# Retention values as a fifth seven-product unit, gate tiles ahead of the stage, and the retention's square sums taken off GpSimd

## What is computed

```python
for l in range(DEPTH):                                   # DEPTH = 2
    x = x + 0.5 * swiglu(rmsnorm(x, norm_ffn1[l]), ...)  # D_FF = 2816
    h = rmsnorm(x, norm_mix[l])
    z = h @ w_in[l]                                      # 1024 x 9728
    rq, rk, rv, rg, dq, dk, dv, g_ret, g_dil = jnp.split(z, IN_SPLITS, axis=-1)
    y_ret = retention(rq, rk, rv, rg, ...) @ w_ret_o[l]  # 4 heads, keys of 128, values of 256
    y_dil = dilated_attention(dq, dk, dv, ...) @ w_dil_o[l]   # 3 groups of 4 heads of 128
    gates = sigmoid(concatenate([g_ret, g_dil], axis=-1) + b_gate[l])
    x = x + (gates[..., :1024] * y_ret + gates[..., 1024:] * y_dil) @ w_out[l]
    x = x + 0.5 * swiglu(rmsnorm(x, norm_ffn2[l]), ...)
# at the end of retention(), for each head:
o = o * lax.rsqrt(jnp.mean(o * o, axis=-1, keepdims=True) + EPS)
return silu(g) * (o * norm_g)
```

## Time and profile before

| what | us |
|---|---|
| median of 3 runs | 2577.52 |
| the profiled execution | 2577.28 |
| its span, first to last instruction | 2575.5 |
| TensorE matmul busy | 2567.7 (100%) |
| VectorE busy | 1936.4 (75%) |
| ScalarE busy | 1121.0 (44%) |
| GpSimd busy | 128.5 (5%) |

### The profile page before, as it was taken

The page is one execution under the profiler, slowest core; times in us unless marked ns, Lnnn a source line. Parts: engine busy times, 40 slices in busy tenths (PEclk is TensorE's granted clock), DMA queues, the critical chain, the costliest instruction groups (busy, mean ns, idle before and its releaser), DMA issues.

```text
span 2575.5 us, 36835 instructions
## 1 busy us (share of the span) xinstructions
PE 2567.7 (100%) x14577; PEld 2255.3 (88%) x14577; DVE 1936.4 (75%) x2430; ACT 1121.0 (44%) x1369; POOL 128.5 (5%) x199
## 2 busy tenths in 40 slices
PE   9999999999999999999999999999999999999999
PEld 7999988888888888999989999888888888889998
DVE  8877866886776679777788777777867766797776
ACT  5433444445655234333443334454466642343332
POOL 1111000110001000000000000011100000000000
PEclk9999999999999999999999999999999999999999
DMA  5433245545443433333223332454554434333331
GB/s 183 150 124 119 66 141 191 175 161 175 138 139 115 164 103 119 103 102 98 99 83 123 98 98 74 173 178 147 172 155 139 138 128 151 115 115 98 103 107 52
DMA packets 201202, 328.98 MB, mean 128 GB/s; under 512 B 15572, under 2 KB 122497, under 8 KB 200525
## 3 DMA queue, kind: packets, MB, share of 16 engines
q1 hardware_dynamic: 186312, 286.35, 34.9%
q0 software_dynamic: 14112, 36.50, 3.9%
q10 hardware_dynamic: 646, 4.31, 0.4%
HBM read 289.11 MB, written 42.64 MB: 129 GB/s over the span
## 4 chain that ended last, share of the span: by engine, by line
PE 99%; DVE 0%; DMA 0%; issue 0%; ACT 0%; ACTq 0%
PE proj L692 23%; PE proj L694 23%; PE proj L693 23%; PE acc L693 9%; PE acc L692 9%; PE acc L694 9%; PE acc L1062 1%; PE acc L988 1%; PE acc L1011 0%; PE acc L970 0%; PE acc L971 0%; PE acc L972 0%; PE acc L1001 0%; PE acc L1000 0%; PE acc L765 0%; PE acc L759 0%
## 5 line engine op out<-in xcount | busy, mean ns | idle before, releaser
L692 PE MATMUL proj<-h_hi,ring_hi 128*128 128x256 f32 (+1 forms) x1632 | 553.4, 339 | 1.8 <-DVE h_lo L1791 1.8
L694 PE MATMUL proj<-h_hi,ring_lo 128*128 128x256 f32 (+1 forms) x1632 | 544.6, 334 | 0.0
L693 PE MATMUL proj<-h_lo,ring_hi 128*128 128x256 f32 (+1 forms) x1632 | 543.7, 333 | 0.0
L692 PE MATMUL proj<-y_hi,ring_hi 128*128 128x256 f32 (+1 forms) x1472 | 450.5, 306 | 0.0
L694 PE MATMUL proj<-y_hi,ring_lo 128*128 128x256 f32 (+1 forms) x1472 | 450.5, 306 | 0.0
L693 PE MATMUL proj<-y_lo,ring_hi 128*128 128x256 f32 (+1 forms) x1472 | 450.5, 306 | 0.0
L1262 ACT ACTIVATE ring_hi<-raw 128x1024 fp32r<-128x1024 f32 (+1 forms) x175 | 209.9, 1203 | 360.3 <-PE acc L694 194.6
L692 PEld LDWEIGHTS proj<-h_hi,ring_hi 128*128 128x128 f32 x1632 | 310.3, 190 | 31.4 <-DVE ring_lo L2572 2.2
L694 PEld LDWEIGHTS proj<-h_hi,ring_lo 128*128 128x128 f32 x1632 | 309.9, 190 | 31.2
L693 PEld LDWEIGHTS proj<-h_lo,ring_hi 128*128 128x128 f32 x1632 | 310.4, 190 | 27.5
L692 PEld LDWEIGHTS proj<-y_hi,ring_hi 128*128 128x128 f32 x1472 | 281.3, 191 | 12.5
(11 more groups left out here) (335 smaller groups left out, 4309.6 us busy)
## 6 DMA issues: line engine op xcount, KB each, us to landing
raw<-in_w_in SPq DMA_DIRECT2D x120, 512.0 KB, 4.7
raw<-in_ffn_gate SPq DMA_DIRECT2D x88, 512.0 KB, 3.7
raw<-in_ffn_up SPq DMA_DIRECT2D x88, 512.0 KB, 4.3
raw<-in_ffn_down SPq DMA_DIRECT2D x56, 512.0 KB, 4.4
qkv_d<-work POOLq DMA_DIRECT2D x72, 256.0 KB, 2.6
work<-in_ffn_down SPq DMA_DIRECT2D x32, 512.0 KB, 5.9
xs<-qkv_d SPq DMA_DIRECT2D x24, 512.0 KB, 6.3
xs<-in_w_in SPq DMA_DIRECT2D x16, 512.0 KB, 5.2
```

The lines of the kernel that those rows point to most:

```text
L692: pe.matmul(o, s_hi, m_hi, start=start, stop=False, skip_group_check=onto)
L693: pe.matmul(o, s_hi, m_lo, start=False, stop=False, skip_group_check=onto)
L694: return pe.matmul(o, s_lo, m_hi, start=False, stop=stop, skip_group_check=onto)
```

## The change

Four things are changed.

- The two blocks of retention values leave the cover and become a fifth unit of seven products, the first of the stage. The cover has one plain block left, and behind it three single tiles of the dilated gates (blocks 2, 4 and 6), which the heads 1 to 3 no longer make: those heads have seven tiles. `norm_sums` stands after 24 matmuls of the cover, `norm_spread` after 48. The results and sums of the cover live in `xs`.
- The small products of heads 1 to 3 are put at other k steps, and the heads' PSUM banks go round.
- `ret_normed`, `ret_gated`, `ret_low` and `ret_out` of the previous head stand at the end of a head, not in its middle; so does the split of the next head's first weights on VectorE.
- The sum of the squares is made by VectorE (`ret_sq_add`), its high part by ScalarE (`ret_sq_high`), its low part by VectorE in the next head (`ret_sq_low`).

```diff
-COVER_BLOCKS, ST_UNITS = 3, 4
-ST_BASE = 2 * COVER_BLOCKS
+ST_BASE, ST_UNITS = 5, 5
+COVER_TILES = (NB, NB, 1, 1, 1)
+COVER_GATES = (2, 4, 6)
+HEAD_TILES = ((2, 2, 2, 2), (2, 2, 1, 2), (2, 2, 1, 2), (2, 2, 1, 2))
...
 SyncE, cover
+                sp.wait_ge(ssq_added, 3 * (N + 1))
+                st_block(l, st_b22[0], 4, ST_COLS[1], b22_landed[0])
+                sp.wait_ge(norm_sum, N + 1)
+                st_block(l, st_b12[0], 0, ST_COLS[1], b12_landed)
...
                 split_of(item + ST_BASE - 2)
                 st_block(l, st_b11, 0, ST_COLS[0], b11_landed)
...
 GpSimd, head
-                pool.wait_ge(ret_o_read, 4 * H + 2)
-                pool.tensor_tensor(ret_sq[0], ret_sq[0], ret_sq[1], ALU.add).then_inc(ret_sq_added, 1)
...
-                pool.tensor_copy(hi, ret_sq[0]).then_inc(ret_sq_hi, 1)
-                pool.wait_ge(ret_sq_hi, H + 1)
-                pool.tensor_tensor(lo, ret_sq[0], hi.bitcast(fp32), ALU.subtract).then_inc(ret_sq_lo, 1)
...
 TensorE, cover
+                        if part == 0 and b == 1:
+                            norm_sums(N)
+                    if part == 0:
+                        norm_spread(N)
+                for b, bank in enumerate((AB[2], AB[3], PB[0])):
+                    u = unit(l, 2 + b)
+                    begin(u)
...
+                    tile_cols(u, bank, 0, width=P)
...
 TensorE, heads 1 to 3
-                    between = ({2: [scores(0), scores(1)]}, {0: [scores(2), scores(3)], 1: [total]}, {2: [move]}, {},
-                               {0: [turn(0), turn(1)], 5: [turn(2), turn(3), values(0), values(1)]},
-                               {1: [values(2), values(3), near_values], 5: [rs(0)]})
+                    between = ({2: [scores(0), scores(1)]}, {0: [scores(2), scores(3)], 1: [total]}, {2: [move]},
+                               {2: [turn(0), turn(1)], 7: [turn(2), turn(3), values(0), values(1)]},
+                               {3: [values(2), values(3), near_values], 7: [rs(0)]})
...
+                    between += ({2: [rs(1)], 3: [kq(0)], 5: [rv(0), rs(2)], 6: [kq(1)]},
+                                {0: [rv(1), rs(3)], 2: [rv(2)], 3: [kq(2)], 4: [kq(3)], 5: [rv(3)], 6: [kq(4)], 7: [kq(5)]})
...
 ScalarE, new
+            def ret_sq_high(H, n):
+                act.wait_ge(ret_sq_added, H + 1)
+                act.wait_ge(ret_pv, 4 * H + 4)
+                act.activation(pt_split(y_hi_flat, n, 0), ret_sq[0], ACT.Copy).then_inc(ret_sq_hi, 1)
...
+            def cover_sigmoid(l, b):
+                act.wait_ge(sxn_ready, SXN * l + KT + b + 1)
...
 ScalarE, end of a head
+                turned(4)
                 ret_squares(H, 0)
                 ret_squares(H, 1)
+                turned(5)
+                gate_silu(H, 0, at(3).tile)
+                if n:
+                    ret_out(H - 1, n - 1, 0)
+                    ret_out(H - 1, n - 1, 1)
                 ret_copy(H, n, 0)
                 ret_copy(H, n, 1)
                 gate_silu(H, 1, at(3).tile + 1)
+                ret_sq_high(H, n)
...
 VectorE, new
+            def ret_sq_add(H):
+                dve.wait_ge(ret_o_read, 4 * H + 2)
+                dve.tensor_tensor(ret_sq[0], ret_sq[0], ret_sq[1], ALU.add).then_inc(ret_sq_added, 1)
...
+            def ret_sq_low(H, n):
+                dve.wait_ge(ret_sq_hi, H + 1)
+                dve.tensor_tensor(pt_split(y_lo_flat, n, 0), ret_sq[0], pt_split(y_hi_flat, n, 0).bitcast(fp32),
+                                  ALU.subtract).then_inc(ret_sq_lo, 1)
...
+            def cover_scale(l, b):
+                done(unit(l, 2 + b).tile)
+                dve.wait_ge(cover_stored[b], 16 * (2 * l + 1))
+                dve.tensor_tensor(cover_gate[b], (AB[2], AB[3], PB[0])[b][:, :], r_b[:, :], ALU.mult).then_inc(sxn_ready, 1)
...
 VectorE, end of a head
                 if more:
                     qk_scale(H + 1)
+                split(at(4))
+                if n:
+                    ret_normed(H - 1)
+                    ret_gated(H - 1)
+                    ret_low(H - 1, n - 1)
+                ret_sq_add(H)
...
 VectorE, merge
                 split(at(M_R0))
+                ret_sq_low(H, RET_HEADS - 1)
                 gated_d(0)
                 gated_d(1)
                 ret_mean(H)
```

More of the change, by code:

```diff
@@ L109, in piece_tile @@
 def piece_tile(layer, u, j):
[L110 removed]
+    return layer * TILES_LAYER + FFN_TILES + sum(COVER_TILES) + 2 * (PROD * u + j)
 def ffn_item(layer, f):
@@ L278, in build, with last_use, head_gates, sg_before @@
         ret_sq = [work[:, 12, :], work[:, 13, :]]
-        t_r, t_seed, t_var, t_b = work[:, 12, :], work[:, 13, :], work[:, 15, :], xs[:, 6, :]
+        t_a, t_seed, t_var, t_b = work[:, 12, :], work[:, 13, :], work[:, 15, :], xs[:, 6, :]
+        t_r = t_var
+        HEAD_BANKS = ((0, 1, 2, 3, 1, 2, 3, 0), (1, 2, 3, 0, 1, 2, 3), (0, 1, 2, 3, 0, 1, 2), (3, 0, 1, 2, 3, 0, 1))
+        def last_use(n, tile):
+            before = [(n - 1, t) for t in range(len(HEAD_BANKS[n - 1]))] if n else []
+            before += [(n, t) for t in range(tile)]
+            return next((h, t) for h, t in reversed(before) if HEAD_BANKS[h][t] == HEAD_BANKS[n][tile])
+        def head_gates(n):
+            return ((0, 0), (1, 0), (0, 1), (1, 1)) if n == 0 else ((0, 2 * n), (0, 2 * n + 1), (1, 2 * n + 1))
+        def sg_before(H):
+            return GATES_OF[RET_HEADS] * (H // RET_HEADS) + GATES_OF[H % RET_HEADS]
+        def sg_uses(H, buffer):
+            n = H % RET_HEADS
+            return (2 * H if buffer == 0 else (RET_HEADS + 1) * (H // RET_HEADS) + n + (n > 0))
+        def head_bank(n, tile):
+            return PB[HEAD_BANKS[n][tile]]
         GD, GR = ([work[:, k, :] for k in of] for of in ((4, 5, 6, 7, 1, 1, 13, 15), (8, 9, 14, 0, 12, 2, 3, 10)))
@@ L376, in two_cols128, with col128 @@
                          (v[:, :, :, P:2 * P], w[:, ds(layer, 1), :, ds(col1, P)])])
+            def col128(u, w, layer, col):
+                v = slot(u, KT * P).rearrange("p o (k c) -> p o k c", c=P)
+                load(u, [(v[:, :, k:k + 4, :], w[:, ds(layer, 1), k:k + 4, ds(col, P)]) for k in (0, 4)])
             def cols512(u, w, layer, col, k0=0):
@@ L1647, in heads @@
                     split(at(2))
+                    dil_exps(H, 2)
+                    dil_exps(H, 3)
+                    swap_halves(H, 1, at(0).tile + 1)
+                    rope_hi(H, 0)
+                    dil_factors(H)
+                    gate_sigmoid(l, n, 0)
+                    gate_sigmoid(l, n, 1)
+                    dil_copy(H, 0)
+                    dil_copy(H, 1)
+                    rope_hi(H, 1)
+                    split(at(3))
+                    dil_copy(H, 2)
+                    dil_copy(H, 3)
+                    dil_out(H, n)
+                    squares(0, 2)
+                    gate_sigmoid(l, n, 2)
+                    scores_hi(H, n, 0)
+                    gate_sigmoid(l, n, 3)
                 else:
```

315 lines of the change are left out of this document (159 added, 156 removed).

## The result

The changed kernel takes **2613.20 us** (median of 4 runs, 2610.39 to 2617.14) against 2577.47 for the kernel before: 1.0140 of its time, 95% interval 1.0122 to 1.0157. It is slower, as forecast, by 35.7 us instead of 22.7, and the time lies 1.2 us above the end of the stated range. The profiled execution took 2610.39 us, 33.1 more than that of before.

The account below looks back on a forecast made before the run. TensorE, 99% of the chain, was taken to bound the kernel: waits of 16.8 us a layer, 33.6 in two, against 10.9 saved gave +22.7, so 2600 us against the median; range 2576 to 2612.

Parts of the forecast that it names:

- what goes: TensorE, both layers: 24 fewer matmuls a layer, 48 in all at 0.2267 us each, saving 10.9 us.
- The sign that went with it: TensorE's matmul busy time should be about 11 us lower in the changed kernel.
- norm sums: Cover: sums now stand after 24 matmuls, so TensorE waits 1.2 us for VectorE's last addition of squares.
- fourth product: Cover, the stage's fourth product: TensorE waits 1.7 us for VectorE's low part; bounds none to 4.
- exchange: Head 1 (`move`): ScalarE's longer list delays exponentials and VectorE's statistics, so TensorE waits 0.85 us.
- exchange in heads 2 and 3: Same list plus `ret_out` and `ret_copy`: exponentials 8.4 us behind the scores, TensorE waits 2.95 us in each head.
- third transpose: Heads 1 and 2 (`kq(2)`): VectorE's chain outlasts 15 matmuls, so TensorE waits 1.25 us each; bounds 0 and 2.
- merge: Merge, sum of squares: TensorE waits 4.65 us for VectorE's low part behind the weights' split; bounds 2.3 and 6.
- nothing waits: Rival for the whole kernel: covers hold everywhere, only the 48 matmuls count, 2566.4 us, faster; chance 0.13.
- the clock held apart as a rival: Rival: six waits all bring a start at the 1.2 GHz level, 1.8 us foretold; slower, chance 0.10.
- upper bounds: Longer waits in cover, heads and merge, 49 us over two layers, bringing the time to 2615 us.
- The heads keep pace: Rival: heads' statistics come in time and the transpose is covered; only cover and merge wait, 2581.5 us; chance 0.15.

Follow-up runs that it names:

- the version without waits: Changed kernel with retention output steps mid-head, keys' factors earlier, squares' low part first in merge, other head-0 banks, later third-gate sigmoid, norm sums 12 matmuls later: 2566.54 us.

## Why the prediction was wrong

**Right: what goes.** 48 matmuls, 10.9 us; the version without waits shows it to 0.1. The sign that went with it did not come: TensorE's matmul busy time is 2568.5 us, not some 11 below 2567.7, since restarts and the lower clock lengthen it.

**Right in place and nearly in size: the foretold waits.** In idle time: norm sums 1.2 foretold, 1.08 and 1.07 in the two layers; fourth product 1.7, 1.32 and 1.39; exchange 0.85, 0.67; exchange in heads 2 and 3 2.95, 2.33 to 2.35; third transpose 1.25, 1.07; merge 4.65, 4.49 (its own numbers give 841.3 + 1.93 + 2.29 + 0.65 - 841.65 = 4.5). Together 28.8 against 33.6. But the prediction reckoned how late TensorE starts, and a row of idle time is 0.16 less than that. With 0.16 for each of 16 foretold waits, and with the 0.3 lost at the third scores of heads 2 and 3 on the way to the exchange, 28.8 becomes 32.6, only 1.0 less than foretold. At the fourth product the chain was right link by link: the stage block there at 392.3 (391.8 foretold), VectorE's queue done at 405.45 (404.9), ScalarE's copy at 408.0 (407.6). At the exchange it was right to 0.1 us.

**Misread, without harm to the sum.** For the cover the prediction took its two numbers one column too far left: VectorE and ScalarE are busy for 43.70 and 26.17 us of 67.10 there, not 55.86 and 43.70. VectorE's share falls short of TensorE's by 23 us, not 11; only a point for "nothing waits" rests on it.

**Failed: the sum.** It added the delays alone and put the banks, and what follows behind a wait, at nothing. Three things were missing in the profiled run. First, 3.4 for the banks of head 0 (3.1 of idle time and 0.16 twice): the change lists that they go round, and the working priced no bank. A tile that takes another bank waits for that bank's last reader, and this is a wait like the others. Second, 1.8 for the slow second matmul behind each of 18 waits. The row with 0.47 us behind 1.81 us of idle shows such a start, at a granted clock of 1.00; the prediction set it beside the clock. Third, and largest, the clock, 6.3. 32.6 + 3.4 + 1.8 + 6.3 - 10.9 makes 33.2, and 33.1 were measured.

**Failed: the clock held apart as a rival.** It stood at 0.10 as a case in which six waits all bring a start at the 1.2 GHz level, held down by the clock of 1.00 throughout the kernel before, where no wait is as long. In truth part of it belonged to the forecast: once TensorE waits 2 to 4 us at several places, some fall, in every run that was profiled with such waits. Its price was near (1.8 foretold from the program's start, 1.58 measured), its number not: four in the profiled run, all behind waits that the rival names. That the median lies 2.8 above the profiled run fits one or two more; that is not shown, since only one run was profiled row by row. The range ended at 2612, below the 2615 of its own upper bounds. These bounds hold longer waits, which did not come; a range up to them would have held the median by luck.

**Rivals.** "The heads keep pace" and "nothing waits" fell, but the second is what the same change gives in another order: 2566.4 stood there, 2566.54 was measured.

## What to carry to other kernels

When TensorE is full, count what stands ahead of each step in the lists of the slower engines, and price every wait with its size, a restart (0.26 us here on top of the idle time) and a share of a stretch at the lower clock (1.6 us here, 2.4 where it was longer). Look for waits in every resource that the diff renumbers, PSUM banks too. A saving that drowns in waits may be whole: take away the cause of each wait, one row at a time, before the idea is given up.

## What the runs showed of the hardware

VectorE's two subtractions of 128x512 took 2.10 us where GpSimd's subtraction ran beside them (849.75 to 851.04, they from 850.09 on), and 1.30 without. This agrees with the Trainium skill ("SBUF — State Buffer", section "Who interferes with whom"), by which a VectorE instruction with two SBUF inputs contends with a GpSimd instruction that reads SBUF.

The granted clock fell behind waits of 4.49, 2.3 and even 1.07 us, yet not behind each of them: of four equal waits of 2.35 in one execution one was followed by it, and in another run it fell within a wait of 4.49. The same program took 2610.39 to 2617.14, while the version without waits stayed within 0.34 us. What decides whether it falls was not settled.

The silu behind a table load starts as the load ends (723.23 + 1.28, then 724.52), and the load as the copy before it ends. The further 1.38 us of draining that the Trainium skill gives ("ScalarE: Activation LUTs", section "What ACT_TABLE_LOAD costs") is not seen here; the measurement decides.
